# One ring of twelve expert tiles in a mixture-of-experts stage on Trainium2: eight slots and four split buffers, with longer loops on TensorE and SyncE

## What is computed

```
def _moe(h, ...):                      # 256 tokens, 32 experts, top 4 of them for each token
    logits = tokens @ w_router + b_router
    top_w = softmax(top_k(logits, 4))
    ...
    hid = tokens[rows] @ w_exp_in[e] + b_exp_in[e]               # 1024 -> 2048
    out = _clamped_swiglu(hid) @ w_exp_out[e] + b_exp_out[e]     # 1024 -> 1024
    y = y.at[row_token].add(out * weight)
```

## Time and profile before

| | us |
|---|---|
| median of 3 runs | 2671.09 (2670.88 to 2671.8) |
| the profiled execution, its own time | 2670.84 |
| its span (first to last instruction) | 2669.0 |
| expert stage (first in-product to the end) | 1731.9 to 2669.0 |

### The profile page before, as it was taken

The page is one execution under the profiler, slowest core; times in us unless marked ns, Lnnn a source line. Parts: engine busy times, 40 slices in busy tenths (PEclk is TensorE's granted clock), DMA queues, the critical chain, the costliest instruction groups (busy, mean ns, idle before and its releaser), DMA issues.

```text
span 2669.0 us, 45584 instructions
## 1 busy us (share of the span) xinstructions
PE 2570.4 (96%) x18038; PEld 2013.9 (75%) x18039; DVE 1586.6 (59%) x2961; ACT 957.5 (36%) x1576; POOL 36.6 (1%) x24
## 2 busy tenths in 40 slices
PE   7999999999999999999999988999999999999998
PEld 5999699899899969989988878855555555555553
DVE  6776666777877666667776776534444434434334
ACT  5444454544544445454454534411111111111111
POOL 0000000000000000000000110000000000000000
PEclk8999999999999999999999998999999999999999
DMA  8654544454444455445444234689999999999997
GB/s 256 239 187 167 207 178 183 166 187 179 169 179 184 169 211 213 178 164 189 184 183 153 95 119 160 259 344 425 430 430 430 430 430 430 430 430 430 430 430 303
DMA packets 70925, 704.58 MB, mean 264 GB/s; under 512 B 11063, under 2 KB 11319, under 8 KB 14343
## 3 DMA queue, kind: packets, MB, share of 16 engines
q1 hardware_dynamic: 65736, 695.11, 64.9%
q0 software_dynamic: 5088, 8.05, 1.4%
HBM read 699.43 MB, written 3.67 MB: 263 GB/s over the span
## 4 chain that ended last, share of the span: by engine, by line
PE 78%; DMA 12%; DVE 7%; ACT 3%; issue 1%; SPq 0%; DVEq 0%; ACTq 0%
PE ps L1719 12%; DMA slot<-in_experts 11%; PE ps L2217 10%; PE ps L1691 9%; PE ps L1694 9%; PE ps L1695 9%; PE ps L1722 6%; PE ps L2241 6%; PE ps L2197 5%; PE ps L2254 2%; DVE u_lo L1018 2%; PE ps L1735 1%; PE ps L1739 1%; PE ps L1738 1%; PE ps L2227 1%
## 5 line engine op out<-in xcount | busy, mean ns | idle before, releaser
L1018 DVE TENSOR_TENSOR u_lo<-ring,u_hi 128x1024 fp32r<-128x1024 f32 x500 | 614.8, 1236 | 309.2 <-ACT u_hi L564 302.3
L564 ACT ACTIVATE u_hi<-ring 128x1024 fp32r<-128x1024 f32 x498 | 523.3, 1056 | 404.5 <-PE ps L1691 219.2
L1719 PE MATMUL ps<-hs,u_hi 128*128 128x512 f32 x1408 | 508.2, 403 | 10.9 <-DVE hs L1044 10.9
L2217 PE MATMUL ps<-slot,xg 128*64 128x256 f32 x4032 | 460.7, 380 | 5.6 <-DMA slot<-in_experts 5.6
L2217 PEld LDWEIGHTS ps<-slot,xg 128*64 128x64 f32 x4032 | 287.6, 137 | 211.0 <-issue 66.3
L1722 PE MATMUL ps<-hs,u_lo 128*128 128x256 f32 x1408 | 397.8, 283 | 0.0
L1719 PEld LDWEIGHTS ps<-hs,u_hi 128*128 128x128 f32 x1408 | 267.4, 190 | 77.0 <-issue 13.1
L1691 PE MATMUL ps<-hs,u_hi 128*128 128x256 f32 x1000 | 290.7, 291 | 6.2 <-DVE hs L1044 5.1
L1694 PE MATMUL ps<-hs,u_hi 128*128 128x256 f32 x1000 | 285.8, 286 | 0.0
L1695 PE MATMUL ps<-hs,u_lo 128*128 128x256 f32 x1000 | 285.6, 286 | 0.0
L1722 PEld LDWEIGHTS ps<-hs,u_lo 128*128 128x128 f32 x1408 | 269.2, 191 | 0.1
(11 more groups left out here) (377 smaller groups left out, 3631.0 us busy)
## 6 DMA issues: line engine op xcount, KB each, us to landing
slot<-in_experts SPq DMA_DIRECT2D x248, 1536.0 KB, 18.8
ring<-in_stream SPq DMA_DIRECT2D x184, 1536.0 KB, 6.4
extra_in<-in_experts SPq DMA_DIRECT2D x4, 1024.0 KB, 11.8
slot<-in_experts SPq DMA_DIRECT2D x4, 1024.0 KB, 5.1
bias<-bias_rows POOLq DMA_DIRECT2D x2, 1280.0 KB, 12.6
konst<-in_konst POOLq DMA_DIRECT2D x1, 2272.0 KB, 14.7
extra_out<-in_experts SPq DMA_DIRECT2D x4, 512.0 KB, 9.4
slot<-in_experts SPq DMA_DIRECT2D x4, 512.0 KB, 15.1
```

Of the source, the lines that this page charges most:

```text
L564: nc.scalar.activation(u_hi[buffer_of(l, k)][:, :], raw_unit(l, k), ACT.Copy).then_inc(unit_hi, 1)
L1018: nc.vector.tensor_tensor(u_lo[b][:, :], raw_unit(l, kk), u_hi[b][:, :].bitcast(F32), ALU.subtract).then_inc(unit_lo, 1)
L1719: mm = mm_(ps[:, bank, :], hi[:, b], src[:, c, :, :], start=c == 0, stop=False, skip_group_check=True)
L2217: mm = mm_(ps[h * CAP:(h + 1) * CAP, j % 2, 0:2 * P], xg[:, b, k * PAIRS + c, :], w[:, at:at + 2 * P], start=k == 0 and c == 0, stop=k == ...
```

## The change

All tiles rotate through twelve places: places 0 to 7 are the slots, places 8 to 11 the split extra buffers. A tile t is in place t mod 12, from the first to the last. The buffers are the same and lie where they did.

- **SyncE**: every tile from 16 on waits for the count t-15 in `moe_used`. A tile for places 8 to 11 is issued as two transfers, 1024 KB and 512 KB. The loop holds two rounds of the ring, 24 tiles (three experts), and has nine iterations; tiles 12 to 23 stand ahead of it, 240 to 259 behind it.
- **TensorE**: with 12 places and 8 tiles an expert the pattern repeats after three experts, and with the two halves of `xg` after six. The loop's body has six `expert_turn`s (`TURNS` = 6) and runs 5 iterations, and the two turns ahead of it are gone: it begins with the turn of expert 0. The instructions that are executed for the products are the same, in the same order.
- `extra_landed` becomes two semaphores, one for places 8 and 9 and one for 10 and 11; before the first tile of such a pair is used, all four transfers of the pair must have landed.
- To free semaphores, those that guard the routing ahead of the experts are merged (`logit_ready`, `wtT_ready` into `route_ready`, `total_taken`, `wtT_taken` into `route_taken`, `max_found`, `sel_ready`, `wt_ready` into `picks_made`); each wait is for the same instruction as before.

```diff
+PLACES = MOE_RING + EXTRA
+TURNS = 6
+LAST_TILE = EXPERTS * DC + EXTRA
+SLOT_USES, EXTRA_USES = LAST_TILE // PLACES + 1, LAST_TILE // PLACES
...
-        def tile_place(e, i):
-
-            if isinstance(e, int) and e < 2 and i < (DC, EXTRA)[e]:
-                return (slots[i], None) if e == 0 else (None, i)
-            return slots[(i + EXTRA) % MOE_RING], None
...
+        def in_rows(r, i):
+            place = (r * DC + i) % PLACES
+            return slots[place][:, IN_PART] if place < MOE_RING else extra_in[place - MOE_RING][:, :]
...
+        def wait_tile(eng, p, g, r, i):
+
+            place, n = (r * DC + i) % PLACES, (r * DC + i) // PLACES + 1
+            if place < MOE_RING:
+                eng.wait_ge(moe_landed[place], (p * SLOT_USES + g * (TURNS * DC // PLACES) + n) * 16)
             else:
-                eng.wait_ge(moe_landed[(i + EXTRA) % MOE_RING], (p * EXPERTS + e + (i >= EXTRA)) * 16)
+                eng.wait_ge(extra_landed[(place - MOE_RING) // 2], (p * EXTRA_USES + g * (TURNS * DC // PLACES) + n) * 64)
...
             def expert_pass(p):
-                for j in range(4):
-                    sp.wait_ge(hid_ready, p * (EXPERTS * PAIRS) + j // 2 + 1)
-                    sp.dma_start(slot(j), experts[DC + 4 + j]).then_inc(moe_landed[j], 16)
-                for j in range(4):
-                    sp.wait_ge(moe_used, p * (EXPERTS * DC) + j + 1)
-                    sp.dma_start(slot(4 + j), experts[2 * DC + j]).then_inc(moe_landed[4 + j], 16)
...
-                    for j in range(4):
-                        sp.wait_ge(moe_used, p * (EXPERTS * DC) + e * DC + (j - 7))
-                        sp.dma_start(slot(j), experts[e * DC + (j + 4)]).then_inc(moe_landed[j], 16)
...
-                with sp.Fori(2, EXPERTS - 1) as e:
-                    rest_of_tiles(e, slice(0, TILE))
-                rest_of_tiles(EXPERTS - 1, OUT_PART)
...
+                def load(place, t):
+                    if place < MOE_RING:
+                        sp.dma_start(slot(place), experts[t]).then_inc(moe_landed[place], 16)
+                    else:
+                        extra_rows(place - MOE_RING, t)
+                        extra_columns(place - MOE_RING, t)
+
+                def load_after_out(t, place):
+                    sp.wait_ge(moe_used, p * (EXPERTS * DC) + t + (1 - PLACES - 4))
+                    load(place, t)
+
+                for t in range(PLACES, PLACES + 4):
+                    sp.wait_ge(hid_ready, p * (EXPERTS * PAIRS) + (t - PLACES) // 2 + 1)
+                    load(t % PLACES, t)
+                for t in range(PLACES + 4, 2 * PLACES):
+                    load_after_out(t, t % PLACES)
+                with sp.Fori(1, EXPERTS * DC // (2 * PLACES)) as h:
+                    for j in range(2 * PLACES):
+                        load_after_out(h * (2 * PLACES) + j, j % PLACES)
...
-                expert_turn(p, 0, 0)
-                expert_turn(p, 1, 1)
-                with pe.Fori(1, EXPERTS // 2 - 1) as e:
-                    expert_turn(p, e * 2, 0)
-                    expert_turn(p, e * 2 + 1, 1)
-                expert_turn(p, EXPERTS - 2, 0, last=True)
+                with pe.Fori(0, (EXPERTS - 2) // TURNS) as g:
+                    for r in range(TURNS):
+                        expert_turn(p, g, r)
+                end = (EXPERTS - 2) // TURNS
+                expert_turn(p, end, 0, last=True)
```

More of the change, by code:

```diff
@@ L346, in build @@
         xtok_copied, y_made = sem("xtok_copied"), sem("y_made")
-        out_made, extra_landed = sem("out_made"), sem("extra_landed")
+        out_made = sem("out_made")
+        extra_landed = [sem(f"extra_landed{i}") for i in range(EXTRA // 2)]
         dve_step = sem("dve_step")
@@ L437, in _, with extra_rows, extra_columns @@
                     sp.dma_start(ring[:, t % RING, :], stream[l * LT + t]).then_inc(tile_landed[t % RING], 16)
[L438 to L442, removed]
+            def extra_rows(i, t=None):
+                sp.dma_start(extra_in[i][:, :], experts[DC + i if t is None else t][:, IN_PART]).then_inc(extra_landed[i // 2], 16)
+            def extra_columns(i, t=None):
+                sp.dma_start(extra_out[i][:, :], experts[DC + i if t is None else t][:, OUT_PART]).then_inc(extra_landed[i // 2], 16)
             for t in range(RING, ST):
@@ new lines, in expert_pass @@
+                for t in range(PLACES, PLACES + 4):
[6 more added lines that the diff above has]
+                        load_after_out(h * (2 * PLACES) + j, j % PLACES)
+                for t in range(EXPERTS * DC // (2 * PLACES) * (2 * PLACES), EXPERTS * DC):
+                    load_after_out(t, t % PLACES)
@@ L497, in _ @@
+                for t in range(EXPERTS * DC, LAST_TILE):
+                    sp.wait_ge(moe_used, p * (EXPERTS * DC) + t + (1 - PLACES - 4))
+                    sp.dma_start(slot(t % PLACES)[:, OUT_PART], experts[t][:, OUT_PART]).then_inc(moe_landed[t % PLACES], 16)
             expert_pass(0)
@@ L932, in _ @@
             take_htok(1)
[L933 removed]
+            a.wait_ge(picks_made, 1)
             for t in range(TT):
@@ L2228, in turn, with expert_out @@
                 mm.then_inc(turned, 1)
-            def expert_out(p, e, j, first=False, last=False):
-                n = p * EXPERTS + e
+            def expert_out(p, g, r, j, first=False, last=False):
+                n = p * EXPERTS + g * TURNS + r
                 pe.wait_ge(eact_ready, n * PAIRS + (j + 1))
@@ L2254, in back, with expert_step @@
                     mm_(ps[:, banks[h], :], placeT[rows, b, t * P:(t + 1) * P], outd[rows, :], start=True, stop=True).then_inc(scat_ready, 1)
-            def expert_step(p, e, j, b, first=False, last=False):
-                n = p * EXPERTS + e
+            def expert_step(p, g, r, j, first=False, last=False):
+                n = p * EXPERTS + g * TURNS + r
                 if j + 2 < PAIRS:
-                    expert_in(p, e, j + 2, b)
+                    expert_in(p, g, r, j + 2)
                 elif not last:
-                    expert_in(p, e + 1, j + 2 - PAIRS, 1 - b)
+                    expert_in(p, g, r + 1, j + 2 - PAIRS)
                 if j < 2 and not first:
-                    back(n - 1, j, 1 - b)
+                    back(n - 1, j, 1 - r % 2)
                 if j == 1 and not last:
@@ L2310, in expert_pass @@
                     rows(1, 5)
-                expert_step(p, EXPERTS - 1, 2, 1, last=True)
-                expert_step(p, EXPERTS - 1, 3, 1, last=True)
+                expert_step(p, end, 1, 2, last=True)
+                expert_step(p, end, 1, 3, last=True)
                 pe.wait_ge(rows_taken, 6)
```

86 lines of the change are left out of this document (36 added, 50 removed).

## The result

The changed kernel took 2681.80 us in the median of 7 runs (2679.60 to 2688.03), the kernel before 2671.62 in 7 runs (2670.14 to 2673.81) beside it. The ratio is 1.0038 with a 95% interval of 1.0028 to 1.0047: slower by 10.2 us. The profiled execution took 2683.12 us, its span is 2681.3.

A forecast was written before the change was run, and what follows sets the result against it. TensorE's work was taken to bound the kernel until about 2208 us, then the transfers. From 2670.84, -9.1 for the ring and +19.2 for four jumps gave 2680.9, with 0.25 for the median 2681 us; range 2664 to 2690.

The forecast's parts named there:

- Case A: TensorE's expert loop: taken jumps miss kept code and the clock falls; net +6.5 to +16.5 us, chance 0.54.
- What bounds the kernel: Expert stage: TensorE's work at 28.66 us an expert until about 2208, then transfers at 29.26 us.
- The ring, -9.1: Twelve places let tiles be issued earlier, so transfers stay ahead and TensorE regains 9.1 us.
- the queue's 10.6 us of lead: Early idle of the data queue, 4.9 and 5.7 us, closes; over 9.1 that leaves a narrow lead of 1.5 us.
- The split transfers: A third of the tiles go as two transfers, costing the queue 0.1 us an expert, 3 us over 30.
- The jump, 4.8 us: Each of four taken jumps of TensorE's expert loop costs 3.1 us of gap and 1.7 of low clock.
- the branch, D: Duration of a taken branch whose target must be fetched beside a full data queue: 5.5 us, between 3.48 and 7.1.
- gap on TensorE: TensorE stands behind each taken jump for the branch time less 2.4 us of queued work: 3.1 us.
- the clock: After each gap TensorE's granted clock is 0.50 for 3.4 us, which costs 1.7 us.
- That 2600 instructions aren't kept: The six-expert loop body on TensorE, 10.2 packets, doesn't stay in instruction memory; chance 0.75.
- Rival C: No stall at TensorE's jumps: -9.1 us, 2662; with packets fetched again each turn -4 us, 2667; chance 0.24.
- The signs: Early stretches at 425 to 430 GB/s, some 120 packets, four branches of 4.6 to 7.1 us, experts of 33 to 35, clock 0.5.

The follow-up runs named there:

- loop of three: Changed kernel with three experts instead of six in TensorE's loop, one xg and three placeT, ScalarE's loop also three: 2663.71 us, ratio 0.9970.
- the loop of three on the old ring: Kernel before, its eight slots kept, with three experts in the loops of TensorE and ScalarE, one xg, three placeT: 2672.77 us, ratio 1.0003.
- the light version: Changed kernel, six experts in TensorE's loop, with 512 columns a transfer for tiles 24 to 239, output not the reference's: 2665.55 us, ratio 0.9976.
- The written-out version: Changed kernel with TensorE's thirty experts written out, so that no branch is taken in them: 2672.61 us, ratio 1.0001.
- the old ring with six: Kernel before, its eight slots kept, with six experts in TensorE's loop (three taken jumps) and experts 26 to 29 written out: 2680.28 us, ratio 1.0030.
- the loop of twelve: Changed kernel with twelve experts in TensorE's loop (one taken jump) and six written out behind it: 2673.57 us, ratio 1.0005.

## Why the prediction was right, point by point

**The time.** Forecast 2681, measured 2681.8. Case A happened: the jumps miss and the clock falls. That the two agree to 0.8 us is in part luck: the terms as the profiles show them come to +12.3, two above the forecast's +10.1, and the medians to +10.2.

**What bounds the kernel.** Right. TensorE at 28.66 us an expert and the queue at 29.26 with a lead that melts are what all ten excesses are built from, with the price of the jumps, and the run with most of the data left out shows the first alone.

**The ring, -9.1.** Right in the changed kernel: no step waits for a transfer, and the 8.58 us of before are gone. But the reason given, that the queue's 10.6 us of lead suffice to the last expert by themselves, held only beside the jumps, which hand the queue 21 us. With the jumps gone the excess is 1.93 us (loop of three) and the ring is worth 6.7 us of excess against before, 7.5 against the loop of three on the old ring, and 7.9 in the medians against before. The split transfers cost 0.12 us an expert (29.38 - 29.26) where 0.1 was the estimate. Over 30 experts that is 3.6 us against the narrow lead of 1.5, so they fit the 1.93 that is left, with about 1.0 of the pairwise wait in it; a version without the split wasn't run.

**The jump, 4.8 us.** Measured 5.2 to 5.3 in all four, term by term:

| term | forecast | measured |
|---|---|---|
| the branch, D | 5.5 | 6.1 |
| gap on TensorE | 3.1 | 3.35 |
| the clock | 1.7 | 1.7 |
| sum | 4.8 | 5.27 |

D was a choice between 3.48 and 7.1, and its reason held: the packet waits behind data, 2.7 us of it. It was set 0.6 too low, and the queued work covered 2.75 us of the branch where 2.4 was taken, which gives 0.35 back. What is left over, 5.27 - 5.05 = 0.2 us a jump, isn't explained; the light version has as much (steps 0.8 to 1.3 us longer for branches of 3.3 and 3.8, less 2.75 of covered time 0.6 and 1.1).

**The sum.** -9.1 + 19.2 = +10.1. The excesses have -8.6 + 21.1 = +12.5, the spans +12.3, the medians +10.2 with an interval of 7.5 to 12.6. The jumps were 1.9 us more than forecast. The ring's 9.1 counted 0.6 behind the last gather, where the excess doesn't look: from there to the end the kernel before took 51.2 us and the changed one 50.4, so that this term was good to 0.3.

**That 2600 instructions aren't kept.** Right, and closer to the edge than said: three experts stay, four don't.

**Rival C, mis-sized.** "If the packets are fetched again in every turn without a stall", it says, "-9.1 shrinks to -4: 2667". The written-out version is that case, and it took 2672.6. The step that failed is the drag of the packets on the data: against "the narrow lead of 1.5 us" packets and split together were put at 5 us of loss. They cost 10.4, of which the packets have 8.5 (10.39 - 1.93). They lengthen eight tiles from 29.38 to 29.53 us, 4.6 us over 30 experts, which meets a lead that the split has already used up. The rest, some 4 us, is not in the mean rate; the parts of a tile that come apart (9.9 us from first to last late in the stage, 2.2 in the loop of three) are of that size and fit it, though no run separates the two. So even without a stall the change, with its packets, would have gained nothing, and part of what the jumps cost is hidden: the four jumps cost 21.1 on TensorE, but only 9.2 against the written-out version, and 18.1 against the loop of three.

**The signs.** All read as named: 427 GB/s in both early stretches, 124 packets, five branch entries with four of 6.1 us, four steps of 34 us, clock 0.50 for 3.4 us after each.

## What to carry to other kernels

Before a loop is lengthened, count the instructions of its body on the engine that sets the time: here TensorE ran bodies up to 1545 again for 0.2 us and paid 5.7 to 6.2 us of branch for each taken jump of one with 1740 or more. If a ring's pattern forces a longer body, first change what else rotates (here `xg` and `placeT`, for the pattern of three) and only then write the loop longer or out, since written-out code costs its packets on a full queue. Where two engines are within 2% of each other, a loss on one is a lead for the other: price each edit in the kernel that it will stand in, not alone.

## What the runs showed of the hardware

- A taken jump out of the kept code took 3.3 to 3.8 us with nearly idle DMA engines and 5.7 to 6.2 us with full ones; the packet started 1.0 us after the branch in the one case and 3.7 in the other (the two kernels with the loop of six on the ring of twelve). Some 2.75 us of that were covered by products already queued.
- Gaps of nearly the same length had three outcomes for the granted clock: no fall (3.1 us, first jump of the old ring with six), 0.50 for 3.4 us (3.1 to 3.4 us, the usual one), 0.50 for 6.8 us (3.3 us, the loop of twelve), worth 0, 1.7 and 3 us.
- The instruction packets of written-out code, 37 in 650 us, 0.61 MB against 276.99 MB of data (0.2%), went with 0.15 us more for eight tiles, 0.5%, and with the sixteen parts of a tile coming apart, up to 11.1 us from the first to the last at the end of the stage. The Trainium skill, in the section named above, says that kernels "prefer full unrolling where possible"; here the written-out version was 8.9 us slower than the loop of three.
- Splitting a third of the tiles into parts of 8 and 4 KB a partition took 0.4% of the queue's rate (eight tiles in 29.38 us against 29.26).
